# Modulation sums over the partitions: 32x32 transposed blocks on VectorE and one matmul per block, in place of 16 or 32 one-column matmuls

## The reference, cut to what matters

```python
c_act = jax.nn.silu(c)
mod = c_act @ w_ada[l] + b_ada[l]                  # [1, 1024] @ [1024, 6144]
...
h = jax.nn.silu(cvec) @ w_mod + b_mod              # [1, 1024] @ [1024, 3072], for cvec = c and cvec = c_ctx
shift, scale, gate = jnp.split(h[:, None, :], 3, axis=-1)
```

## Time and profile before

| what | us |
|---|---|
| median of 3 runs | 2634.71 |
| lowest and highest run | 2628.62, 2650.54 |
| span of the profiled execution | 2636.3 |
| TensorE busy in it | 2487.7 |
| VectorE busy in it | 1342.4 |

### The profile page before, as it was taken

The page is one execution under the profiler, slowest core; times in us unless marked ns, Lnnn a source line. Parts: engine busy times, 40 slices in busy tenths (PEclk is TensorE's granted clock), DMA queues, the critical chain, the costliest instruction groups (busy, mean ns, idle before and its releaser), DMA issues.

```text
span 2636.3 us, 29001 instructions
## 1 busy us (share of the span) xinstructions
PE 2487.7 (94%) x11544; PEld 1937.1 (73%) x11544; DVE 1342.4 (51%) x1509; ACT 652.8 (25%) x948; POOL 733.3 (28%) x492
## 2 busy tenths in 40 slices
PE   6999889999999999999998799999998999989998
PEld 3776656666678888888786478885586778878876
DVE  6556754437524344344435879996428321324423
ACT  3002334423411101100123611114215100035510
POOL 1241320035552233232345022110145232240011
PEclk9999989999999999999999799999999999999999
DMA  6652000222232232233232031113232531110021
GB/s 222 209 160 70 21 19 9 74 71 84 68 104 88 80 99 86 76 100 96 72 96 80 16 104 38 40 32 116 73 120 80 163 76 48 48 40 1 1 88 72
DMA packets 228851, 206.96 MB, mean 79 GB/s; under 512 B 15248, under 2 KB 203280, under 8 KB 227712
## 3 DMA queue, kind: packets, MB, share of 16 engines
q1 hardware_dynamic: 223552, 178.61, 22.5%
q10 hardware_dynamic: 3840, 21.89, 2.1%
q0 software_dynamic: 1344, 4.91, 0.5%
HBM read 180.35 MB, written 17.83 MB: 75 GB/s over the span
## 4 chain that ended last, share of the span: by engine, by line
PE 78%; DVE 9%; ACT 4%; issue 4%; PEld 2%; DMA 1%; POOL 1%; PEldq 1%; SPq 0%; ACTq 0%; DVEq 0%; POOLq 0%
PE G L1663 28%; PE G L304 26%; PE M L307 2%; PE G L1151 2%; PE M L3047 2%; PE G L2552 1%; PE M L400 1%; PE M L1698 1%; PE G L2368 1%; PE M L2368 1%; DVE WMAX L3070 1%; ACT WPT L3108 1%; PE G L2395 1%; PE M L2554 1%; PEldq L3202 1%
## 5 line engine op out<-in xcount | busy, mean ns | idle before, releaser
L278 POOL TENSOR_SCALAR WH<-RAW 128x1024 fp32r<-128x1024 f32 (+1 forms) x156 | 134.7, 863 | 939.5 <-PE G L1663 515.8
L304 PE MATMUL G<-HH,WH 128*128 128x512 f32 x1056 | 337.8, 401 | 10.4 <-DVE HL L488 4.0
L304 PE MATMUL G<-HL,WH 128*128 128x512 f32 x1056 | 333.4, 397 | 0.0
L304 PE MATMUL G<-HH,WL 128*128 128x512 f32 x1056 | 333.2, 397 | 0.0
L281 POOL TENSOR_TENSOR WL<-RAW,WH 128x1024 fp32r<-128x1024 f32 (+1 forms) x156 | 304.2, 1950 | 13.0
L1663 PE MATMUL G<-HH,WH 128*128 128x512 f32 x624 | 220.5, 403 | 13.5 <-POOL WL L281 4.7
L304 PEld LDWEIGHTS G<-HH,WH 128*128 128x128 f32 x1056 | 188.7, 189 | 57.9 <-issue 11.8
L304 PEld LDWEIGHTS G<-HL,WH 128*128 128x128 f32 x1056 | 189.1, 189 | 42.4
L304 PEld LDWEIGHTS G<-HH,WL 128*128 128x128 f32 x1056 | 189.1, 189 | 42.3
L1663 PE MATMUL G<-HL,WH 128*128 128x512 f32 x624 | 217.3, 398 | 0.0
L1663 PE MATMUL G<-HH,WL 128*128 128x512 f32 x624 | 217.0, 398 | 0.0
(11 more groups left out here) (544 smaller groups left out, 4413.9 us busy)
## 6 DMA issues: line engine op xcount, KB each, us to landing
RAW<-in_w_ff SPq DMA_DIRECT2D x40, 512.0 KB, 3.9
RAW<-in_w_ff SPq DMA_DIRECT2D x80, 256.0 KB, 2.8
WVEC<-in_w_ada SPq DMA_DIRECT2D x24, 512.0 KB, 4.8
FVEC<-in_e_w_mod SPq DMA_DIRECT2D x24, 512.0 KB, 3.9
FVEC<-in_o_w_mod SPq DMA_DIRECT2D x24, 512.0 KB, 3.7
RAW<-in_o_w_in SPq DMA_DIRECT2D x24, 512.0 KB, 3.7
RAW<-in_e_w_in SPq DMA_DIRECT2D x20, 512.0 KB, 3.6
ADA<-in_w_ada SPq DMA_DIRECT2D x4, 2048.0 KB, 19.6
```

Source lines behind the costliest of these rows:

```text
L278: pool.tensor_scalar(hi, raw, 1.0, 0.0, ALU.mult, ALU.add).then_inc(w_high, 1)
L304: m = pe.matmul(G[s][:, n * w:(n + 1) * w], part[s][:, k, :], acts[i][:, k, n * w:(n + 1) * w], start=first, stop=last)
```

## The change

VectorE reduces each sum tile with a transposing reduction: every 32x32 block of the tile (32 partitions, 32 columns) is transposed and then summed, so that a 128x1024 tile becomes 128x32 (tile PART): partition 32q + r of column c holds the sum over the 32 partitions of quarter q of output column 32c + r. One f32 matmul adds the four quarters: its weights are LANES, a fixed 128x128 matrix with a one where row and column agree modulo 32, and PART's 32 columns (64 for two vectors) are the moving operand. add() reads the result as four groups of 32 partitions and becomes four instructions. LANES is made once from IDENT at the start of stage "win". mod_part now counts one for each reduction and mod_read four for each block, and the waits on them are rescaled. MOD_COL moves from 1000 to 960 to make room for 64 columns.

```diff
--- before.py
+++ after.py
@@ -197,6 +197,8 @@
         SEL = at("SEL", [P, 2 * P], F32, sel_at)
         IDR = at("IDR", [P, P], F32R, sel_at + kb)
         MMX = at("MMX", [P, 16], F32R, bns_at)
+        LANES = at("LANES", [P, P], F32, sel_at + kb + kb // 2)
+        PART = at("PART", [P, 2, 2, 32], F32, bns_at)
         z0 = small[0]
         assert base + z0 + 144 * kb <= 229368, base + z0 + 144 * kb
 
@@ -345,7 +347,7 @@
 
 
 
-        MOD_COL = 1000
+        MOD_COL = 960
 
         class Modulation:
 
@@ -387,30 +389,29 @@
                 dve.wait_ge(S("mod_row"), self.rows_done)
                 dve.sem_inc(vec_used[g % 2], 1)
                 if k == KT - 1:
-                    dve.sem_inc(S("mod_part"), 1)
+                    for x in range(len(xs)):
+                        dve.tensor_reduce(PART[:, b % 2, x, :], self.sums_of(b)[x].rearrange("p (c j) -> p c j", j=32), AX.X,
+                                          ALU.add, apply_transpose=True).then_inc(S("mod_part"), 1)
 
             def sum(self, pe, b):
-                xs = self.blocks[b][4]
-                pe.wait_ge(S("mod_part"), b + 1)
+                n = len(self.blocks[b][4])
+                pe.wait_ge(S("mod_part"), n * (b + 1))
                 if b >= 2:
-                    pe.wait_ge(S("mod_read"), b - 1)
-                for j in range(KT):
-                    for x in range(len(xs)):
-                        c = MOD_COL + j * len(xs) + x
-                        m = pe.matmul(M[b % 2][:, c:c + 1], self.sums_of(b)[x][:, j * P:(j + 1) * P], ONES[:, 0:1],
-                                      start=True, stop=True)
-                m.then_inc(S("mod_sum"), 1)
+                    pe.wait_ge(S("mod_read"), 4 * (b - 1))
+                pe.matmul(M[b % 2][:, MOD_COL:MOD_COL + 32 * n], LANES[:],
+                          PART[:, b % 2, 0:n, :].rearrange("p x c -> p (x c)"), start=True, stop=True)\
+                  .then_inc(S("mod_sum"), 1)
 
             def add(self, dve, b):
                 _, bias, j, dst, xs = self.blocks[b]
                 dve.wait_ge(S("mod_sum"), b + 1)
-                got = M[b % 2][:, MOD_COL:MOD_COL + KT * len(xs)]
-                if len(xs) == 1:
-                    dve.tensor_tensor(dst, got, vec(bias, j, KT), ALU.add).then_inc(S("mod_read"), 1)
-                else:
-                    dve.tensor_tensor(dst, got.rearrange("p (a b) -> p a b", b=2),
-                                      vec(bias, j, KT).unsqueeze(2).broadcast_to([P, KT, 2]), ALU.add)\
-                       .then_inc(S("mod_read"), 1)
+                n = len(xs)
+                got = M[b % 2][:, MOD_COL:MOD_COL + 32 * n].rearrange("p (x f q) -> p q f x", x=n, q=4)
+                to = dst.unsqueeze(2) if n == 1 else dst
+                add = vec(bias, j, KT).unsqueeze(2).broadcast_to([P, KT, n])
+                for q in range(4):
+                    r = slice(32 * q, 32 * q + 32)
+                    dve.tensor_tensor(to[r], got[r, q], add[r], ALU.add).then_inc(S("mod_read"), 1)
 
         def ada_block(j):
             return ("w_ada", "b_ada", j, MODA[:, j:j + KT], [CACT[:]])
@@ -643,6 +644,11 @@
 
         def win_dve(dve):
             u0 = info("win")["u0"]
+            dve.tensor_reduce(LANES[:, 0:32], IDENT[:].rearrange("p (q i) -> p i q", q=4), AX.X, ALU.add)\
+               .then_inc(S("lanes"), 1)
+            dve.wait_ge(S("lanes"), 1)
+            dve.tensor_copy(LANES[:, 32:P].rearrange("p (q i) -> p q i", q=3),
+                            LANES[:, 0:32].unsqueeze(1).broadcast_to([P, 3, 32])).then_inc(S("lanes"), 1)
             for j in range(16):
                 for q in (2 * j, 2 * j + 1):
                     WMOD.rows(dve, q)
@@ -662,7 +668,7 @@
                 if j >= 14:
                     latent_norm(dve, j - 14)
             WMOD.add(dve, 3)
-            dve.wait_ge(S("mod_read"), 4)
+            dve.wait_ge(S("mod_read"), 16)
             dve.tensor_scalar(MODA[:, 32:40], MODA[:, 32:40], 1.0, 1.0 / ALPHA, ALU.add, ALU.mult).then_inc(S("one_plus"), 1)
 
         def win_act(act):
@@ -696,15 +702,17 @@
             for j in range(16):
                 if j:
                     gemm_unit(pe, j % 2, (u0 + j) // 2, SEQ, (HH, HL))
+                if j == 4:
+                    pe.wait_ge(S("lanes"), 2)
                 if j in (4, 8, 12):
                     WMOD.sum(pe, j // 4 - 1)
                 if j == 13:
                     pe.wait_ge(S("lat_add"), 1)
-                    pe.wait_ge(S("mod_read"), 2)
+                    pe.wait_ge(S("mod_read"), 8)
                     ones_sum(pe, M[1], SEQ, [LSQ[0]]).then_inc(S("lat_ms"), 1)
                 if j == 14:
                     pe.wait_ge(S("lat_sq"), 3)
-                    pe.wait_ge(S("mod_read"), 3)
+                    pe.wait_ge(S("mod_read"), 12)
                     ones_sum(pe, M[0], SEQ, [LSQ[1]]).then_inc(S("lat_ms"), 1)
             pe.wait_ge(S("lat_sd"), 1)
             WMOD.sum(pe, 3)
@@ -1701,7 +1709,7 @@
         def context_turn_pe(pe):
 
             pe.wait_ge(ct_in, 32)
-            pe.wait_ge(S("mod_read"), len(FMOD.blocks))
+            pe.wait_ge(S("mod_read"), 4 * len(FMOD.blocks))
             for f in range(KT):
                 for t in range(2):
                     c0 = CTX * (f % 4) + t * P
@@ -1831,7 +1839,7 @@
             for u in A_AT:
                 if u[1] in range(1, LAST) or u[1] == 0 and u[3] == 1:
                     feed(u)
-            act.wait_ge(S("mod_part"), len(FMOD.blocks))
+            act.wait_ge(S("mod_part"), 2 * len(FMOD.blocks))
             for t in range(2):
                 act.dma_start(CT[:, t, :], A["ctx"][t * P:(t + 1) * P, :]).then_inc(ct_in, 16)
             feed(("a", LAST, 0, 0))
@@ -2013,7 +2021,7 @@
                    .then_inc(S("en_lo"), 1)
 
             def gains():
-                dve.wait_ge(S("mod_read"), len(FMOD.blocks))
+                dve.wait_ge(S("mod_read"), 4 * len(FMOD.blocks))
                 for l, (mod, gain) in enumerate(((MODE, "e_norm"), (MODO, "o_norm"))):
                     for c in range(2):
                         dve.scalar_tensor_tensor(out=GS[:, l, :, c], in0=mod[:, 8:16, c], scalar=1.0,
```

## The result

The changed kernel takes 2601.11 us in the median of four runs (2598.45 to 2609.17); the kernel before, with a fourth run added to the three shown ahead of the prediction, 2641.22 (2628.62 to 2650.54). The ratio is 0.9853, 95% interval 0.9817 to 0.989, so 1.5% faster. The forecast was 2597.8 and 1.4%. The profiled execution's span went from 2636.3 to 2597.6 us, its own time is 2599.37: 1.8 us lie around the span.

The account below looks back on a forecast made before the run. TensorE's own instructions bound the kernel (busy 94%). Removing 23.1 (FMOD sums), 9.95 (clock falls), 2.9 and 0.96 us (WMOD), 36.9 in all, from the 2634.71 us median gives 2597.8 us, 1.4% less; range 2589 to 2616.

Parts of the forecast that it names:

- The chain of matmuls in wf: Stage wf, from 764.21 us: matmuls only, so FMOD's six one-column blocks, 24.4 us, lie on the path; 23.1 us less.
- The price of the new matmul: Each block's sum on TensorE: one f32 matmul with 64 (32) columns costs 0.22 us; ends 0.21 and 0.5.
- The clock: Product matmuls behind FMOD's six sums: clock falls cost 9.95 us there, all gone with the change.
- rival A: FMOD sums in wf: the clock falls stay, only 23.3 us come off in all, 2611.4 us; chance 0.12.
- WMOD, blocks 1 and 2: Stage win, sums at 158.99 and 205.57 on the chain: 2 x (1.68 - 0.22) = 2.9 us less.
- WMOD, block 0: Stage win, sum at 111.28: nothing gained, since unit 7's weight split at 131.76 had waited for its DMA.
- WMOD, block 3: End of stage win: sum cheaper by 1.47 us, three more VectorE adds of 0.17; 0.96 us less, ends nothing and 1.5.
- The reductions: VectorE, 16 transposing reductions of 128x1024 behind the row products: 1.2 us each, far end 6.55, hidden from TensorE.
- The free room of 2.66 us per x: FMOD blocks, between last row products and eviction: each reduction may take 2.66 us; each microsecond above costs 2 us per block.
- Rival B: GpSimd's weight splits in wf are stretched by reductions, TensorE waits; 5 to 10 us given back, 2605 us; chance 0.10.
- Rival C: Reductions before the eviction take 6.55 us each: 13.7 us slower, 2648 us; loses from 5.7 us on; chance 0.04.
- Rival D: The sums do not lie on the path as the chain says; time moves by less than 5 us; chance 0.02.

Follow-up runs that it names:

- spread: Kernel before, with FMOD's one-column matmuls issued in groups between the next unit's products instead of in one run; ratio 0.9963, FMOD stretch 481.3 us.
- wide: Kernel before, with each of FMOD's one-column matmuls given 128 columns of ones, still in one run; ratio 0.9952, FMOD stretch 481.3 us.
- w_only: Kernel before with the change in stage win alone (WMOD new, FMOD old); ratio 0.9964, FMOD stretch 490.6 us.
- look_before: Kernel before, unedited, run once more for a second profile; FMOD stretch 493.7 us, six clock falls.
- f_only: Kernel before with the change in stage wf alone (FMOD new, WMOD keeping one-column matmuls); ratio 0.9859, FMOD stretch 461.2 us.
- reduce_x4: Changed kernel with every FMOD reduction done four times, with waits between; ratio to the kernel before 1.0013, FMOD stretch 504.1 us.
- after_again: Whole changed kernel run once more, unedited, beside the partial ones; ratio to the kernel before 0.9853, FMOD stretch 461.2 us.
- look_after: Changed kernel, unedited, run once more for a further profile; FMOD stretch 461.1 us, no clock falls.

## Why the prediction was right, point by point

- The chain of matmuls in wf. Right, and the reason why the forecast could be made to the microsecond: on an unbroken chain of one engine, what was removed came off. 33.05 us were forecast for wf (23.1 + 9.95), 34.2 measured.
- The price of the new matmul. Forecast 0.22 us by line 1720, measured 0.17 with 64 columns and 0.14 with 32. Over eight sums on the path that is 0.5 us more gained.
- The clock. The 9.95 us forecast for the products behind the sums came off, and a little more: 7.2 behind blocks 1 to 4 (365.8 - 4 x 89.65), 2.1 behind block 5, 1.6 behind block 6, 10.9 in all. The price at full clock was taken a little high, 0.2340 per product against 0.2335. Priced whole, rival A's difference to the forecast was 13.6 us; spread and wide measured 14.1. What the prediction did not see: "All six blocks are followed by such a fall" is so in this trace, not in every one. w_only has five, and look_before's six cost 1.6 us less than before's.
- WMOD, blocks 1 and 2. Forecast 2.9, measured 3.1.
- WMOD, block 0. Forecast nothing, since unit 7 waits for a DMA; with w_only unit 7's split starts at 131.87 against 131.76: nothing.
- WMOD, block 3. Forecast 0.96, measured 2.09 - 1.13 = 0.96. That it is the same to the hundredth is luck: the matmul was 0.07 us cheaper than forecast, and the adds dearer, 0.19 us from one start to the next in place of 0.17. VectorE at that place after, against the earlier trace rows: the reduction ends at 234.00 where the reciprocal starts at 233.92, with no idle time left. The reciprocal comes 1.3 us behind the row products, 1.14 before: 0.2 us late where "fits to within 0.1" was forecast, and nobody waits for it.

```profile
232.75 1.25 DVE L393 TRANSPOSE_TENSOR_REDUCE PART<-X 128x32 f32<-128x1024 f32 x1
233.92 6.51 DVE L639 RECIPROCAL X<-X 128x1024 f32<-128x1024 f32 x1
...
243.32 0.74 DVE L414 TENSOR_TENSOR MODA<-M,V 32x8 f32<-32x8 f32 x4 [1.57 <-PE M L401]
244.09 0.17 DVE L672 TENSOR_SCALAR MODA<-MODA 128x8 f32<-128x8 f32 x1
```

- A clock fall that the prediction did not see. It looked at the sum behind unit 8 and took win's shorter sums as without a fall. Behind the fourth one, at the stage's end, the clock does fall in before, look_before and f_only, not in spread and wide, which have the same matmuls there. TensorE's first eight matmuls behind it, in before and in wide:

```profile
246.78 5.37 PE L744 MATMUL M<-RQ,SWAPR 128*128 128x512 f32 x8 [0.71 <-DVEq L3202]
246.64 3.67 PE L748 MATMUL M<-RQ,SWAPR 128*128 128x512 f32 x8 [0.74 <-DVEq L3206]
```

  The fall costs these eight 1.7 us. In all seven profiles with the new sums in win they take 3.67, though TensorE idles longer ahead of them, 1.3 us. So the idle time alone does not bring this fall; whether the run of eight alone would was not tried.

- The reductions. Forecast 1.2 us, measured 1.20 to 1.25, and hidden. The free room of 2.66 us per x held in blocks 1 to 5 (2.55 us per x: nothing lost) and was too large for block 6, where slower row products come before it. The Trainium skill ("Vector Engine (DVE) Microarchitecture Reference", section 3.8 "The reshape front-end and per-opcode configuration") says that the transposing front-end keeps up one element per cycle and lane, an estimate of some 1.1 us for 1024 elements. The trace agrees, with 1.20 to 1.25.
- Rival A fell with the profile after, which has no fall in the stretch; spread and wide show what the falls hung on. In reduce_x4 the clock fell behind waits of 3.64 us, in the kernel before behind sums in which TensorE was busy throughout. The Trainium skill ("TensorE: Matmul & The Clock Gate", section "HAM oscillation — how this bites in real kernels") asks that TensorE has no long idle gaps. By reduce_x4 the trace agrees; the busy runs of one-column matmuls it does not tell of, and there the traces decide.
- Rival B fell: the split at 860.65 took 2.94 us, as before, and TensorE came 1.5 us after its end. Rival C's place and point were right, its price too low by the clock's share: the gain was gone at 5.1 us per reduction (reduce_x4), not at 5.7. Rival D fell with f_only.
- The sum in win: 3.9 forecast, 5.0 with w_only, but only 2.6 to 3.9 in the three profiles of the changed kernel (181.4 to 182.7 us against 185.3), where the second WVEC load comes later. No step of the prediction had this, and it is not explained.
- The total. Forecast 36.9 us; the medians differ by 40.1, the first pair of profiles by 38.7. The 38.7 are 34.2 in the FMOD stretch, 0.3 ahead of it and 4.2 behind it. So in this pair hardly any of win's gain is left at the start of the stretch. Over all profiles it is there: the first 408 products end at 859.7 to 864.5 us in the five with the old sums in win (mean 862.2), at 856.7 to 860.7 in the seven with the new ones (mean 858.6), 3.6 us sooner. The 4.2 us behind the stretch are less than what one kernel differs by from one profile to the next: there the changed kernel's profiles took 1277.1, 1292.1 and 1281.6 us to the end, the two of before 1281.3 and 1291.3. 34.2 + 3.6 = 37.8 us is the estimate from this of what the change removes, 0.9 more than forecast; that the median lies within 3.3 us of the forecast is in part luck.

## What to carry to other kernels

Look at the granted clock by windows beside every odd little stretch on TensorE, also where it is never idle: here runs of one-column matmuls cost their own time and then some of their neighbours'. Sixteen matmuls with 128 columns in place of one cost only 0.1 us more here, and spreading the small ones among the large kept the clock up. And where one engine's chain is unbroken, a change is worth just what it removes from that chain, as long as each thing that it adds elsewhere meets its deadline on the chain. Work the deadline out for each block, since past it the loss was the wait and the clock.

## What the runs showed of the hardware that was not expected

A run of 32 records of one-column f32 matmuls, 3.5 us with TensorE busy throughout, was followed by the lower clock level (1.2 GHz) in 22 of 24 cases over four profiles; the same run with 128 columns never, in six. The runs of eight in win (1.68 us) were followed by it in 3 of 20 cases over five profiles, each time behind the fourth, where TensorE also idles for 0.7 us. Sixteen f32 matmuls with one column took 3.46 us at the full clock, with 128 columns 3.57.

The largest difference between profiles of one kernel lies where stage wa begins, almost 1000 us behind the FMOD stretch: there the record of the clock has one low stretch of 34.1 us in after_again and look_before and one of 6.8 us in after and look_after. The windows over it in after and in after_again:

```profile
2306.00:2340.00 34.00, 30.00 (x226) 27.84 (x227) 14.38 (x30) 19.34 (x41) 17.91 (x11) 0.90 0.12 33
```

```profile
2307.00:2341.00 34.00, 31.97 (x152) 31.12 (x152) 8.57 (x20) 14.65 (x31) 18.12 (x11) 0.51 0.11 34
```

With 0.51 against 0.90 of the clock over 34 us, the first profile of after and that of after_again, the same kernel, differ by 12.6 us in span while their FMOD stretches agree to 0.1 us. A single execution of this kernel can thus be off by a third of what this change gave; the medians of the kernel before on record go from 2634.67 (19 executions) to 2641.22 (four).
